# Four known experts in one job, and fewer rounded slots for the last main tiles, in a two-block transformer kernel with a mixture of experts

## The chip, the cores and the metric

One core of one Trainium2 chip runs the whole program. The metric is device time in microseconds (us) of one execution. TensorE (PE) multiplies, VectorE (DVE), ScalarE (ACT) and GpSimd (POOL) do the rest, and the queue of SyncE (SP) issues nearly all loads.

## The reference

Two blocks work on 256 tokens of width 1024. The first has two layers with feed-forward networks, a convolution mixer, an mLSTM mixer and cross attention. The second has a mixer with three branches, an output product, a layer norm, and then the part that matters here: a router, 16 experts of which each token takes two, and an embedding term gated by a product with `ple_gate`.

```
h = layer_norm_2(DEEPNORM_ALPHA_2 * h + y, ln1_g, ln1_b)        # y = merged @ w_out
e = (p @ ple_proj) * sigmoid(h @ ple_gate)
aff = sigmoid(h @ w_router)                                     # 16 columns
# the best of 4 groups of 4 experts, then the best 2 experts in it; weights from aff, normed
m = sum over the 2 experts of w * (silu(h @ gate_e) * (h @ up_e)) @ down_e
out = layer_norm_2(DEEPNORM_ALPHA_2 * h + m + e, ln2_g, ln2_b)
```

An expert has 1024 x 1024 floats of `gate` and `up` and 512 x 1024 of `down`. All is float32.

## The kernel before

**Main tiles.** All weights ahead of the experts come as a fixed list of tiles (`weight_tiles`), most of them 128 x 2048 floats, 1 MiB. SP loads tile `i` into one of four `raw` buffers (`load`). ScalarE rounds it into `whi` (`round_tile`) and VectorE makes the rest, `raw - whi`, in `wlo` (`rest_tile`), each in two halves; TensorE multiplies with both. There are four rounded slots, tile `i` in slot `i % 4`, and both engines wait before they write it until TensorE is through with tile `i - 4`. Rounding is called from a `Stream` that stands in each engine's own order of work and runs two or three tiles ahead.

The last main tiles are, in order: two of `mla_proj_2`, two of `conv_proj_2` (the second is `out2_0 - 1`), four of `w_out_2` (`out2_0` to `out2_0 + 3`) and `ple_proj_2`. The output product takes tile `out2_0`, then `+1`, each for both blocks of 128 tokens. Then it takes `+2` and `+3` together (`tail=True`): both for the first token block, then both for the second. For tile `out2_0 + j` it waits for `merged j`. VectorE makes these in pairs: in its order stand the rounding of tiles `out2_0 + 1` and `+2`, then the sums of columns 2 and 3, then `merged` 2 and 3, then the rounding of `+3` and of the `ple` tile.

**After the output product.** A layer norm in two token blocks gives `x`. TensorE turns block 0 (`turned(7, 0)`), multiplies the embedding (`embedded(t, n)`), and for the router turns block 1 and takes 16 columns (`affinities(t)`). VectorE's `route` picks experts, and `placing` finds each token's slot in its expert.

**Experts.** Four experts are known in advance (`FIXED`, columns 0 to 3, experts 12 to 15); the other twelve are ranked by their number of tokens at run time (columns 4 to 15). Each column has room for a fixed number of tokens (`ROOM`). If a column has more, a flag starts further passes over everything (`PASSES`); with these inputs the known ones have 22, 16, 23 and 27 tokens, the ranked ones 66, 51, 51, 45, 40, 36, 30, 27, 27, 26, 16 and 9. A job fills the 128 partitions with the slots of two or four experts (`PIECES`). For each job: `gather` brings its tokens' columns (for two jobs at a time), four `up` steps make gate and up products, then ScalarE's silu, VectorE's product (`gated`), a transpose (`turn_h`), a selection (`columns`), two `down` steps and two `scatter` steps back to the tokens. Between them stand four products `gate(c)` for the embedding. Products with experts of one job go to different columns of TensorE (64 or 32 each) and run side by side.

**Expert tiles.** Each expert has six tiles of 1 MiB (four for `up`, two for `down`), and there are four gate tiles. `expert_tiles` gives the order. They go round 15 slots (`wslots`), and four more slots are used once (`ONCE`). A slot's first load waits for what lay there (`wslot_after`), a later one for the step that used it (`used`). SP issues them in the order of its list and waits for each in turn; four go out in the middle of the last main tiles, the others after `merged 3`, behind the router's weights `wr`. The last norm's row `gbv` is the last load.

Of the kernel before, what the change touches and what calls it, by code (L numbers as in the profile page):

```python
# [10 lines left out]
D = 1024  # L11
T = 256
FF = 2816
NEXP = 16
# [6 lines left out]
TILE = 2048  # L21
# [102 lines left out]
NR, NS, LOOK, OPEN = 4, 4, 2, 0  # L124
# [4 lines left out]
RANKED = NEXP - FIXED  # L129
HALVES = [[(0, 64, q), (64, 128, q + 1)] for q in (0, 2, 5, 7, 9)]  # L130
PIECES = HALVES + [[(32 * i, 32 * i + 32, 4) for i in range(3)] + [(96, 128, 11)], [(32 * i, 32 * i + 32, 12 + i) for i in range(4)]]
ROOM = 4 * [64] + [96] + 6 * [64] + 5 * [32]
JOBS, PASSES = len(PIECES), 4
WSLOTS = 15
LATE = (2 * 512, 3 * 512, 4 * 512)
ONCE = (0, 8, 12, 17)
EROWS = 768
# [10 lines left out]
def group_jobs(G):  # L148
    return range(2 * G - 1, 2 * G + 1) if G else range(1)

# [168 lines left out]
def program(nc, A, out):  # L319
# [5 lines left out]
    with ctx:  # L325
# [80 lines left out]
        prior = [i - NR if i >= NR else None for i in range(main_tiles)]  # L406
        out2_0 = next(i for i, t in enumerate(tiles) if t[0] == "w_out_2")
        etiles = [expert_tiles(v == 0) for v in range(PASSES)]
        enumber = [{t: i for i, t in enumerate(tiles_)} for tiles_ in etiles]
# [106 lines left out]
        pTr = kT[:, 0, :, :]  # L516
        pp = blocks(ar[:, 0:2 * D], D)

        def held(i):
            return [hold[h * NS + i % NS][:, :] for h in range(2)]  # L520

        m4 = main_tiles - 4
        wslots = [ar[:, 2 * D + TILE * i:2 * D + TILE * (i + 1)] for i in range(3)]
        wslots += [raw[(m4 + i) % NR][:, :] for i in range(2)] + held(m4) + [raw[(m4 + 2 + i) % NR][:, :] for i in range(2)]
        wslots += held(m4 + 1) + held(m4 + 2) + held(m4 + 3)
        wslot_after = [None] * 3 + [("raw", m4), ("raw", m4 + 1)] + [("tile", m4)] * 2 + [("raw", m4 + 2), ("raw", m4 + 3)]
        wslot_after += [("tile", m4 + 1 + i) for i in range(3) for h in range(2)]
        assert len(wslots) == len(wslot_after) == WSLOTS
        wslots += [xe[:, 0, :, :].rearrange("p b n -> p (b n)"), r[:, :, :].rearrange("p t d -> p (t d)"), hs[:, :], gbv]

        arena = Arena(ar, 2 * D + 3 * TILE)
        sel16 = vm[:, :, :, :].rearrange("p a b n -> p (a b n)")[0:16].rearrange("p (q n) -> p q n", n=64)
# [41 lines left out]
        def tile_views(i):  # L574
            t = tiles[i]
            w, n = tile_width(t), t[5] - t[4]
            return blocks(whi[i % NS][:, 0:w], n), blocks(wlo[i % NS][:, 0:w], n)

# [17 lines left out]
        def tensor(e):  # L596
# [563 lines left out]
            embedded(0, 0)  # L1160
            embedded(0, 1)
            affinities(0)
            turned(7, 1)
            embedded(1, 0)
            affinities(1)
# [182 lines left out]
        def scalar(e):  # L1348
# [8 lines left out]
            def round_tile(i):  # L1357
                t = tiles[i]
                made = whi_made
                if i >= NS:  # L1360
                    need.wait_ge(*pe.at("tile", i - NS))
                for n in range(len(part_cuts(t)) - 1):
                    c0, c1 = part_cols(i, n)
                    if i == 0:
                        need.wait_ge(*xT_in[n].at("xT"))
                        copy(xhi[:, 2 * n:2 * n + 2, :], xTr[:, 2 * n:2 * n + 2, :]).then_inc(*act.up(("xhi", 0, n)))
                    need.wait_ge(*(piece_in[i][n] if i < 2 else raw_in[slot[i]]).at("raw", i))
                    copy(whi[i % NS][:, c0:c1], raw_t[slot[i]][:, c0:c1]).then_inc(*made.up((i, n)))

            w = Stream(round_tile, main_tiles)  # L1370

# [446 lines left out]
            tokens(0)  # L1818
            embedded(0, 1)
            turned(7, 1)  # L1820
            embedded(1, 0)
            tokens(1)
            need.wait_ge(*pe.at("bank", ("router",)))
            e.activation(aff, blocks(place["router",][:, 0:32], 16), ACT.Sigmoid).then_inc(*act.up(("aff",), took(("router",))))
            embedded(1, 1)
            normed(7)
            gate_part(0)

            def experts(v, s):
# [22 lines left out]
                def take(n, i):  # L1852
                    need.wait_ge(*s.pe.at("bank", ("ey", v, n, i)))
                    if n:
                        need.wait_ge(*s.pe.at("back", v, n - 1, i, 1))
                    if (v, n, i) == (0, 0, 0):
                        need.wait_ge(*pe.at("used", 0, 0, 5))
                    copy(y_hi[:, 512 * i:512 * i + 512], place["ey", v, n, i][:, :]).then_inc(*s.act.up(("yhi", v, n, i)))
# [53 lines left out]
        def vector(e):  # L1912
# [5 lines left out]
            def rest_tile(i):  # L1918
                hi_made, made = whi_made, wlo_made
                if i >= NS:  # L1920
                    need.wait_ge(*pe.at("tile", i - NS))
                for n in range(len(part_cuts(tiles[i])) - 1):
                    c0, c1 = part_cols(i, n)
                    if i == 0:
                        rest(xlo[:, 2 * n:2 * n + 2, :], xTr[:, 2 * n:2 * n + 2, :], xhi[:, 2 * n:2 * n + 2, :],
                             ("xhi", 0, n)).then_inc(*dve.up(("xT", 0, n)))
                    need.wait_ge(*hi_made.at(i, n))
                    e.tensor_tensor(wlo[i % NS][:, c0:c1], raw_t[slot[i]][:, c0:c1], whi[i % NS][:, c0:c1].bitcast(f32),  # L1928
                                    ALU.subtract).then_inc(*made.up((i, n)))

            w = Stream(rest_tile, main_tiles)

# [604 lines left out]
            def experts(v, s, part=range(JOBS + 1), amid=None):  # L2537
# [32 lines left out]
                def columns(n):  # L2570
                    need.wait_ge(*s.pe.at("bank", ("pbc", v, n)))
                    if n > 1:
                        need.wait_ge(*s.pe.at("back", v, n - 2, 1, 1))
                    i = 0 if n < len(HALVES) else n - len(HALVES) + 1
                    col = slot_col[:, i:i + 1]
                    e.tensor_scalar(tsel[:, n % 2, :], place["pbc", v, n][:, 0:256], col, None,
                                    ALU.is_equal).then_inc(*s.dve.up(("T", v, n), took(("pbc", v, n))))
# [160 lines left out]
        def gpsimd(e):  # L2738
# [92 lines left out]
            then(e.memset(roomT, 64.0))  # L2831
            for q in (4, *range(11, 16)):
                then(e.memset(room[:, q:q + 1], float(ROOM[q])))
# [3 lines left out]
            then(e.affine_select(out=roomT, in_=roomT, compare_op=ALU.is_ge, fill=32.0, base=10, pattern=[[0, 1]],  # L2837
                                 channel_multiplier=-1))
            pool.mark("roomT")
            then(e.memset(sel16, 0.0))  # L2840
# [14 lines left out]
        def sync(e):  # L2855
# [12 lines left out]
            def load_expert(v, i, late=None):  # L2868
# [7 lines left out]
                if g == ONCE[0]:  # L2876
                    need.wait_ge(*pe.at("bank", ("rstd",)))
                elif g == ONCE[1]:
                    need.wait_ge(*dve.at("centred", 7, 1))
                    need.wait_ge(*act.at("sq", 7, 1))  # L2880
                elif g == ONCE[2]:
                    need.wait_ge(*pe.at("tile", main_tiles - 1))
                elif g == ONCE[3]:
                    for t in range(2):
                        need.wait_ge(*dve.at("x", 7, t, 1))
                elif turn_of[g] >= WSLOTS:
                    v_, i_ = esequence[ring[turn_of[g] - WSLOTS]]
                    need.wait_ge(*(over if v_ else main).pe.at("used", v_, *[etiles[v_][i_][m] for m in (0, 2)]))
                elif wslot_after[turn_of[g]] is None:
                    need.wait_ge(*pe.at("bank", ("rstd",)))  # L2890
                elif wslot_after[turn_of[g]][0] == "raw":
                    i_ = wslot_after[turn_of[g]][1]
                    need.wait_ge(*wlo_made.at(i_, len(part_cuts(tiles[i_])) - 2))
                else:
                    need.wait_ge(*pe.at(*wslot_after[turn_of[g]]))
# [24 lines left out]
            for i in range(NR, main_tiles):  # L2920
# [15 lines left out]
                if i == out2_0:  # L2936
                    for n in range(4):
                        load_expert(0, n)
            need.wait_ge(*dve.at("merged", 3))
            e.dma_start(wr, blocks(A["wr"][:, :], NEXP)).then_inc(*router_in.up(("router",)))  # L2940
            for i in (*range(4, 8), 9, 10, 11, 13, 14, 8, 15, 17, 16, 18, 12, *range(19, len(etiles[0]))):
                load_expert(0, i)
            for late in range(2):
                for i in range(len(etiles[0]) - len(job_columns(JOBS - 1)), len(etiles[0])):
                    load_expert(0, i, late)
            n, _, j = etiles[0][ONCE[3]]
            need.wait_ge(*pe.at("used", 0, n, j))
# [141 lines left out]
```

## Time and profile before

| | us |
|---|---|
| median of 3 runs | 1460.66 (1460.21 to 1463.91) |
| profiled execution, its own time | 1460.58 |
| its span | 1458.8 |
| PE busy | 1426.8 (98%) |
| PE weight load busy | 1160.8 (80%) |
| DVE busy | 915.1 (63%) |
| ACT busy | 710.1 (49%) |
| POOL busy | 50.1 (3%) |

The span is from the first to the last instruction of one profiled execution; its own time is 1.8 us more. Busy times of engines overlap. In the chain that ended last, PE has 91% of the span and DVE 5%. The engines are told apart by stage below: an average over the span says little, since the transfers run at 229 GB/s in the mean and above 400 GB/s in the expert stage.

### The profile page before, as it was taken

To read this page: it belongs to the slowest core of one execution; us is meant where nothing else is said; L and a number is where in the kernel's file an instruction comes from. 1 tells how busy PE (TensorE), PEld (TensorE's weight loads), DVE (VectorE), ACT (ScalarE), POOL (GpSimd) and SP (SyncE) were. 2 spreads that over 40 slices of the span, in tenths; PEclk is the share of its full clock that TensorE was granted. 3 is DMA by queue.
4 is the path that set the end of the run, shared out by engine and by line. 5 is a ranking of instruction groups with operands and counts; after the bars stand their busy time and mean duration, and the time that the engine had idled before them with its cause. 6 is when DMAs were issued, how large, how long until landed. Compare 5 with 4: busy or idle time off the path is not lost.

```text
span 1458.8 us, 20739 instructions
## 1 busy us (share of the span) xinstructions
PE 1426.8 (98%) x8376; PEld 1160.8 (80%) x8376; DVE 915.1 (63%) x1510; ACT 710.1 (49%) x1185; POOL 50.1 (3%) x116
## 2 busy tenths in 40 slices
PE   8999999999999999999999999998999999999995
PEld 7888888888888988889888888888899997445441
DVE  7666678766666765566677656667989686121123
ACT  7445456455564554455754554545557663112111
POOL 0000000000000000000022000001000012000000
PEclk9999999999999999999999999999999999999998
DMA  9754554564545555545336645553563479999997
GB/s 345 279 202 173 190 205 154 202 231 174 195 180 188 210 183 207 194 148 180 135 116 245 251 176 182 193 175 133 177 202 117 144 303 409 388 412 421 417 421 296
DMA packets 50198, 333.78 MB, mean 229 GB/s; under 512 B 5808, under 2 KB 6064, under 8 KB 12208
## 3 DMA queue, kind: packets, MB, share of 16 engines
q1 hardware_dynamic: 48512, 322.55, 59.3%
q10 hardware_dynamic: 1584, 9.83, 1.8%
q8 instruction: 68, 1.11, 0.3%
q14 instruction: 34, 0.28, 0.1%
HBM read 331.31 MB, written 1.05 MB: 228 GB/s over the span
## 4 chain that ended last, share of the span: by engine, by line
PE 91%; DVE 5%; ACT 1%; DMA 1%; SPq 1%; POOL 1%; issue 0%; DVEq 0%; ACTq 0%
PE psw L602 56%; PE psy L602 33%; PE psw L605 2%; DVE wlo L1928 1%; SPq L2873 1%; DMA hold<-in_we 1%; POOL r L2790 0%; DVE x L2020 0%; DVE kT L2319 0%; DVE xs L1937 0%; ACT whi L1355 0%; ACT gb L1477 0%; DMA ar<-in_xT 0%; DVE r L2002 0%; DVE x L2033 0%
## 5 line engine op out<-in xcount | busy, mean ns | idle before, releaser
L602 PE MATMUL psw<-xs,whi 128*128 128x512 f32 (+2 forms) x2160 | 650.5, 366 | 6.5 <-DVE wlo L1928 6.4
L1928 DVE TENSOR_TENSOR wlo<-raw,whi 128x1024 fp32r<-128x1024 f32 (+4 forms) x415 | 476.8, 1192 | 77.6 <-ACT whi L1355 72.5
L602 PE MATMUL psw<-xs,wlo 128*128 128x256 f32 x1848 | 484.4, 280 | 0.0
L602 PEld LDWEIGHTS psw<-xs,whi 128*128 128x128 f32 (+1 forms) x2160 | 375.9, 189 | 61.8 <-DVE wlo L1928 6.4
L1355 ACT ACTIVATE whi<-raw 128x1024 fp32r<-128x1024 f32 (+4 forms) x415 | 402.3, 1024 | 7.7 <-PE psy L602 5.2
L602 PEld LDWEIGHTS psw<-xs,wlo 128*128 128x128 f32 x1848 | 350.3, 190 | 17.2
L1355 ACT ACTIVATE hf<-psw 128x256 f32<-128x256 f32 x90 | 34.1, 385 | 211.8 <-PE psw L602 211.7
L1973 DVE TENSOR_TENSOR hf<-hf,psw 128x256 f32<-128x256 f32 x82 | 34.0, 420 | 146.9 <-ACT hf L1355 146.9
L1355 ACT ACTIVATE ar<-psw 128x256 f32<-128x256 f32 (+2 forms) x141 | 60.0, 430 | 126.3 <-PE psw L602 124.3
L602 PE MATMUL psy<-whi,hhi 128*128 128x512 f32 x352 | 111.1, 390 | 0.0
L602 PE MATMUL psy<-wlo,hhi 128*128 128x512 f32 x352 | 111.0, 389 | 0.0
L602 PE MATMUL psy<-whi,hlo 128*128 128x512 f32 x352 | 111.0, 389 | 0.0
L602 PEld LDWEIGHTS psy<-wlo,hhi 128*128 128x128 f32 x352 | 66.1, 188 | 13.8
L602 PEld LDWEIGHTS psy<-whi,hlo 128*128 128x128 f32 x352 | 66.1, 188 | 13.8
L602 PEld LDWEIGHTS psy<-whi,hhi 128*128 128x128 f32 x352 | 66.1, 188 | 12.8 <-issue 0.2
L1980 DVE TENSOR_TENSOR ar<-ar,psw 128x256 f32<-128x256 f32 x82 | 34.2, 417 | 52.4 <-ACT ar L1355 52.4
L602 PE MATMUL psy<-hold,r 128*32 128x512 f32 (+1 forms) x272 | 52.1, 621 | 2.2 <-DMA hold<-in_we 2.2
L2748 POOL TENSOR_TENSOR rstd<-ve,mhalf 128x1 f32<-128x1 f32 x18 | 11.9, 662 | 1111.6 <-DVE ve L2026 1111.6
L2319 DVE SCALAR_TENSOR_TENSOR kT<-ar,par,kT 128x256 f32<-128x256 f32 x120 | 49.7, 477 | 0.0
L602 PE MATMUL psw<-whi,xs 128*128 128x256 f32 (+1 forms) x224 | 47.7, 302 | 0.6 <-DVE xs L1937 0.6
L602 PE MATMUL psy<-whi,xs 128*128 128x384 f32 (+1 forms) x192 | 45.1, 340 | 0.8 <-DVE xs L1937 0.8
L1355 ACT ACTIVATE hhi<-psw 128x512 fp32r<-128x512 f32 x17 | 10.0, 597 | 70.3 <-PE psw L602 64.8
(347 smaller groups left out, 1786.5 us busy)
## 6 DMA issues: line engine op xcount, KB each, us to landing
raw<-in_ws SPq DMA_DIRECT2D x189, 1024.0 KB, 4.8
hold<-in_we SPq DMA_DIRECT2D x47, 1024.0 KB, 10.9
raw<-in_we SPq DMA_DIRECT2D x22, 1024.0 KB, 9.5
ar<-in_we SPq DMA_DIRECT2D x20, 1024.0 KB, 10.9
gb<-in_ln ACTq DMA_DIRECT2D x7, 1024.0 KB, 5.0
raw<-in_ws SPq DMA_DIRECT2D x9, 768.0 KB, 4.3
raw<-in_ws SPq DMA_DIRECT2D x4, 672.0 KB, 4.0
raw<-in_ws SPq DMA_DIRECT2D x8, 256.0 KB, 7.0
```

The source lines that it names most:

```text
L602: return e.matmul(o, l, rr, start=start, stop=stop)
L605: return e.transpose(o, i, ident[0:n, 0:n])
L1355: return e.activation(o, i, ACT.Copy, **k)
L1928: e.tensor_tensor(wlo[i % NS][:, c0:c1], raw_t[slot[i]][:, c0:c1], whi[i % NS][:, c0:c1].bitcast(f32), ALU.subtract).then_inc(*made.up((i, ...
L1973: e.tensor_tensor(hf[:, s, j, :], hf[:, s, j, :], place["fgate", f, c, j][:, 0:256], ALU.add).then_inc(*dve.up(("fgate", f, c, j), took((" ...
L1980: then(e.tensor_tensor(corr[j], corr[j], place["up", f, c, j][:, 0:256], ALU.add), took(("up", f, c, j)))
L2319: ins = e.scalar_tensor_tensor(out=ca[:, b, :], in0=zc[:, b, tap:tap + 256], scalar=dwt[:, b, tap:tap + 1], in1=ca[:, b, :], op0=ALU.mult, ...
L2748: e.tensor_tensor(rstd[:, t:t + 1], ve[:, t:t + 1], mhalf[:, 0:1], ALU.pow).then_inc(*pool.up(("rstd", n, t)))
L2873: e.dma_start(wslots[at][:, c0:c1], A["we"][bass.ds(rows_of[q] + 128 * j, 128), c0:c1] if q in rows_of else A["we"][0:128, c0:c1]).then_in ...
```

## The change

The first job takes all four known experts, 32 slots each, in place of two jobs of two with 64 slots each. There are six jobs instead of seven, and their room shrinks with them. `PASSES` goes from 4 to 8. The rounded slots of the last main tiles are laid out by hand: `out2_0 + 2` takes the slot of `out2_0`, `+3` that of `+1`, the `ple` tile that of `out2_0 - 2`; the `ple` tile is rounded before `+3`. The slot of `out2_0 - 1` is then free for two expert tiles, and the embedding's product `pp` moves from `ar` into a used slot, so that `ar` holds four expert tiles instead of three. Five expert tiles are loaded early, four more follow before the wait for `merged 3`. The router's two products stand one behind the other.

```diff
+PIECES = [quarters(0), halves_of(5), halves_of(7), halves_of(9), [(32 * i, 32 * i + 32, 4) for i in range(3)] + [(96, 128, 11)], quarters(12)]
+KIND = (2, 0, 0, 0, 1, 2)
+ROOM = 4 * [32] + [96] + 6 * [64] + 5 * [32]
+JOBS, PASSES = len(PIECES), 8
...
-ONCE = (0, 8, 12, 17)
+ONCE = (0, 14, 15, 16)
+EARLY_SLOTS = 5
...
+        m_ple = out2_0 + 4
+        hslot, hprior = [i % NS for i in range(main_tiles)], [i - NS if i >= NS else None for i in range(main_tiles)]
+        spare = hslot[out2_0 + 3]
+        for i, taken in ((out2_0 + 2, out2_0), (out2_0 + 3, out2_0 + 1), (m_ple, out2_0 - 2)):
+            hslot[i], hprior[i] = hslot[taken], taken
+        making = list(range(main_tiles))
+        making[out2_0 + 3], making[m_ple] = m_ple, out2_0 + 3
...
+        pp = blocks(held(hslot[out2_0 + 2])[0], D)
+        wslots = [ar[:, TILE * i:TILE * (i + 1)] for i in range(4)] + held(spare)
+        wslots += [raw[slot[i]][:, :] for i in (out2_0 + 1, out2_0 + 2, m_ple, out2_0 + 3)]
+        wslots += [held(hslot[out2_0 + 2])[1], *held(hslot[out2_0 + 3]), *held(hslot[m_ple])]
+        wslot_after = [None] * 4 + [("tile", out2_0 - 1)] * 2 + [("raw", i) for i in (out2_0 + 1, out2_0 + 2, m_ple, out2_0 + 3)]
+        wslot_after += [("tile", out2_0 + 2), ("tile", out2_0 + 3), ("tile", out2_0 + 3), ("tile", m_ple), ("tile", m_ple)]
...
+            embedded(1, 0)
+            turned(7, 1)
             affinities(0)
-            turned(7, 1)
-            embedded(1, 0)
             affinities(1)
             embedded(1, 1)
...
                 if i >= NS:
-                    need.wait_ge(*pe.at("tile", i - NS))
+                    need.wait_ge(*pe.at("tile", hprior[i]))
...
-                    copy(whi[i % NS][:, c0:c1], raw_t[slot[i]][:, c0:c1]).then_inc(*made.up((i, n)))
+                    copy(whi[hslot[i]][:, c0:c1], raw_t[slot[i]][:, c0:c1]).then_inc(*made.up((i, n)))
...
-            w = Stream(round_tile, main_tiles)
+            w = Stream(lambda i: round_tile(making[i]), main_tiles)
...
             embedded(1, 1)
+            tokens(1)
...
-            for q in (4, *range(11, 16)):
+            for q in (*range(5), *range(11, 16)):
                 then(e.memset(room[:, q:q + 1], float(ROOM[q])))
...
+            then(e.affine_select(out=roomT, in_=roomT, compare_op=ALU.is_ge, fill=32.0, base=-4, pattern=[[0, 1]],
+                                 channel_multiplier=1))
...
                 if i == out2_0:
-                    for n in range(4):
+                    for n in range(EARLY_SLOTS):
                         load_expert(0, n)
-            need.wait_ge(*dve.at("merged", 3))
-            e.dma_start(wr, blocks(A["wr"][:, :], NEXP)).then_inc(*router_in.up(("router",)))
-            for i in (*range(4, 8), 9, 10, 11, 13, 14, 8, 15, 17, 16, 18, 12, *range(19, len(etiles[0]))):
+            for i in range(EARLY_SLOTS, len(etiles[0])):
+                if i == EARLY_SLOTS + 4:
+                    need.wait_ge(*dve.at("merged", 3))
+                    e.dma_start(wr, blocks(A["wr"][:, :], NEXP)).then_inc(*router_in.up(("router",)))
                 load_expert(0, i)
```

VectorE's `rest_tile` changes as ScalarE's `round_tile` does. The new helpers `quarters(q)` and `halves_of(q)` give the pieces of a job of four and of two experts.

## Rows read from the trace of the kernel before

**Rows 1.** Windows: stretch, length, each engine's busy time, clock, DMA share, GB/s.
```profile
1234.60:1280.00 45.40, 45.40 (x248) 19.00 (x246) 8.94 (x28) 5.76 (x10) 0.00 (x0) 1.00 0.96 378
1280.00:1420.00 140.00, 140.00 (x864) 63.52 (x860) 28.64 (x54) 25.02 (x35) 0.00 (x0) 1.00 1.01 420
1420.00:1446.00 26.00, 18.64 (x122) 6.34 (x120) 5.71 (x11) 1.79 (x3) 0.00 (x0) 0.87 1.01 406
```

**Rows 2.** Chain of waits, expert stage: start, duration, what.
```profile
1297.14 2.06 PE psw L602 x8
1299.20 7.02 PE psy L602 x32
1306.22 0.59 PE psw L605 x4
1306.81 3.58 PE psy L602 x16
1310.39 7.59 PE psw L602 x36
...
1434.98 10.65 DMA hold<-in_we
```

**Rows 3.** Timeline of the SP queue: start, duration of the group, issues.
```profile
1163.02 0.33 SPq L2911 DMA_DIRECT2D xe<-in_wg  x1
1163.39 1.71 SPq L2911 DMA_DIRECT2D ar<-in_we  x3
1165.14 17.52 SPq L2864 DMA_DIRECT2D raw<-in_ws  x4
1195.30 0.33 SPq L2940 DMA_DIRECT2D ar<-in_wr  x1
...
1220.43 0.43 SPq L2911 DMA_DIRECT2D hs<-in_we  x1
1234.60 4.74 SPq L2911 DMA_DIRECT2D ar<-in_we  x3
```

**Rows 4.** Timeline of TensorE, one `up` step of four experts (two records each).
```profile
1370.15 3.64 PE L602 MATMUL psy<-hold,r 128*32 128x512 f32 x32
```

**Rows 5.** Windows, columns as in rows 1: transfers starting from an empty queue.
```profile
1163.00:1165.50 2.50, 2.50 (x23) 2.50 (x23) 1.22 (x1) 2.47 (x5) 0.00 (x0) 1.00 0.57 134
```

**Rows 6.** Timeline of ScalarE: rounding of `+1` and `+2`; copies of block 1's transpose.
```profile
1185.53 3.89 ACT L1355 ACTIVATE whi<-raw 128x1024 fp32r<-128x1024 f32 x4
...
1213.65 1.09 ACT L1355 ACTIVATE xe<-psw 128x512 f32<-128x512 f32 x2 [1.09 <-PE psw L605]
```

**Rows 7.** Timeline of TensorE: start of tile `+2`, and the first transpose after the product.
```profile
1196.76 0.62 PE L602 MATMUL psy<-whi,mhi 128*128 128x512 f32 x2
...
1207.65 1.03 PE L605 MATMUL psw<-par,x 128*128 128x128 f32 x8
```

**Rows 8.** Timeline of VectorE: roundings, `merged` 2 and 3, and `pick(0)`.
```profile
1186.61 4.63 DVE L1928 TENSOR_TENSOR wlo<-raw,whi 128x1024 fp32r<-128x1024 f32 x4 [0.26 <-ACT whi L1355]
...
1193.80 1.47 DVE L1937 TENSOR_TENSOR mlo<-ar,mhi 128x512 fp32r<-128x512 f32 x2
...
1196.06 4.63 DVE L1928 TENSOR_TENSOR wlo<-raw,whi 128x1024 fp32r<-128x1024 f32 x4 [0.18 <-ACT whi L1355]
...
1225.54 0.74 DVE L2551 TENSOR_SCALAR gsel<-ar 128x64 fp32r<-128x64 f32 x4
```

**Rows 9.** Timeline of TensorE: 8 router products as 16 records, and the first gather.
```profile
1211.28 1.85 PE L602 MATMUL psy<-ar,xe 128*128 128x16 f32 x16
...
1227.10 0.52 PE L602 MATMUL psw<-gsel,mhi 128*128 128x128 f32 x2
```

**Rows 10.** Last job: two of TensorE's waits (in brackets), and the clock after the first.
```profile
1424.74 5.29 PE L602 MATMUL psy<-hold,r 128*32 128x512 f32 x32 [2.24 <-DMA hold<-in_we]
1431.63 0.63 PE L605 MATMUL psw<-par,hf 128*128 128x128 f32 x4 [1.59 <-DVE hf L2567]
...
1424.70:1428.10 3.40, 3.36 (x16) 0.90 (x20) 0.00 (x0) 0.00 (x0) 0.00 (x0) 0.50 1.01 419
```

More of the change, by code:

```diff
@@ L129, with quarters, halves_of @@
 RANKED = NEXP - FIXED
[L130 to L133, printed above, removed]
+def quarters(q):
+    return [(32 * i, 32 * i + 32, q + i) for i in range(4)]
+def halves_of(q):
+    return [(0, 64, q), (64, 128, q + 1)]
+PIECES = [quarters(0), halves_of(5), halves_of(7), halves_of(9), [(32 * i, 32 * i + 32, 4) for i in range(3)] + [(96, 128, 11)], quarters(12)]
+KIND = (2, 0, 0, 0, 1, 2)
+ROOM = 4 * [32] + [96] + 6 * [64] + 5 * [32]
+JOBS, PASSES = len(PIECES), 8
 WSLOTS = 15
 LATE = (2 * 512, 3 * 512, 4 * 512)
-ONCE = (0, 8, 12, 17)
+ONCE = (0, 14, 15, 16)
+EARLY_SLOTS = 5
 EROWS = 768
@@ L148, in group_jobs @@
 def group_jobs(G):
-    return range(2 * G - 1, 2 * G + 1) if G else range(1)
+    return range(2 * G - 1, min(2 * G + 1, JOBS)) if G else range(1)
 def group_of(n):
@@ L516, in program, with held @@
         pTr = kT[:, 0, :, :]
[L517 to L527, printed above, removed]
+        def held(k):
+            return [hold[h * NS + k][:, :] for h in range(2)]
+        pp = blocks(held(hslot[out2_0 + 2])[0], D)
[4 more added lines that the diff above has]
+        wslot_after += [("tile", out2_0 + 2), ("tile", out2_0 + 3), ("tile", out2_0 + 3), ("tile", m_ple), ("tile", m_ple)]
         assert len(wslots) == len(wslot_after) == WSLOTS
-        wslots += [xe[:, 0, :, :].rearrange("p b n -> p (b n)"), r[:, :, :].rearrange("p t d -> p (t d)"), hs[:, :], gbv]
-        arena = Arena(ar, 2 * D + 3 * TILE)
+        wslots += [xe[:, 0, :, :].rearrange("p b n -> p (b n)"), r[:, :, :].rearrange("p t d -> p (t d)"), gbv, hs[:, :]]
+        arena = Arena(ar, 4 * TILE)
         sel16 = vm[:, :, :, :].rearrange("p a b n -> p (a b n)")[0:16].rearrange("p (q n) -> p q n", n=64)
@@ L576, in tile_views @@
             w, n = tile_width(t), t[5] - t[4]
-            return blocks(whi[i % NS][:, 0:w], n), blocks(wlo[i % NS][:, 0:w], n)
+            return blocks(whi[hslot[i]][:, 0:w], n), blocks(wlo[hslot[i]][:, 0:w], n)
         def part_cols(i, n):
@@ L1819, in scalar @@
             embedded(0, 1)
+            embedded(1, 0)
             turned(7, 1)
-            embedded(1, 0)
-            tokens(1)
             need.wait_ge(*pe.at("bank", ("router",)))
@@ L1855, in take @@
                         need.wait_ge(*s.pe.at("back", v, n - 1, i, 1))
-                    if (v, n, i) == (0, 0, 0):
-                        need.wait_ge(*pe.at("used", 0, 0, 5))
                     copy(y_hi[:, 512 * i:512 * i + 512], place["ey", v, n, i][:, :]).then_inc(*s.act.up(("yhi", v, n, i)))
@@ L1920, in rest_tile @@
                 if i >= NS:
-                    need.wait_ge(*pe.at("tile", i - NS))
+                    need.wait_ge(*pe.at("tile", hprior[i]))
                 for n in range(len(part_cuts(tiles[i])) - 1):
@@ L1927, in rest_tile @@
                     need.wait_ge(*hi_made.at(i, n))
-                    e.tensor_tensor(wlo[i % NS][:, c0:c1], raw_t[slot[i]][:, c0:c1], whi[i % NS][:, c0:c1].bitcast(f32),
+                    e.tensor_tensor(wlo[hslot[i]][:, c0:c1], raw_t[slot[i]][:, c0:c1], whi[hslot[i]][:, c0:c1].bitcast(f32),
                                     ALU.subtract).then_inc(*made.up((i, n)))
-            w = Stream(rest_tile, main_tiles)
+            w = Stream(lambda i: rest_tile(making[i]), main_tiles)
             def rest(lo, src, hi, event, scale=None):
@@ L2573, in columns @@
                         need.wait_ge(*s.pe.at("back", v, n - 2, 1, 1))
-                    i = 0 if n < len(HALVES) else n - len(HALVES) + 1
-                    col = slot_col[:, i:i + 1]
+                    col = slot_col[:, KIND[n]:KIND[n] + 1]
                     e.tensor_scalar(tsel[:, n % 2, :], place["pbc", v, n][:, 0:256], col, None,
@@ L2881, in load_expert @@
                 elif g == ONCE[2]:
-                    need.wait_ge(*pe.at("tile", main_tiles - 1))
-                elif g == ONCE[3]:
                     for t in range(2):
                         need.wait_ge(*dve.at("x", 7, t, 1))
+                elif g == ONCE[3]:
+                    need.wait_ge(*pe.at("tile", m_ple))
                 elif turn_of[g] >= WSLOTS:
@@ L2945, in sync @@
                     load_expert(0, i, late)
-            n, _, j = etiles[0][ONCE[3]]
+            n, _, j = etiles[0][ONCE[2]]
             need.wait_ge(*pe.at("used", 0, n, j))
```

## The prediction

> **What bounds the kernel now.** I read the profile from its end backwards. The windows come first [rows 1]: from 1280 us to 1420 us TensorE is busy throughout and the DMA engines are full as well, at 420 GB/s; after 1420 us TensorE is busy 18.64 us of 26 us while the DMA engines stay full to 1446 us. Two resources run side by side, and the reader should see which of them ends last. The chain of waits says it [rows 2]: the last long piece before the final norm is the landing of a `hold` slot, 1434.98 us plus 10.65 us. So the end is set by the transfers: the last expert tile lands near 1445.6 us, and some 13 us of products, norm and store follow.
>
> When can that last tile land? The expert stage loads 16 x 6 expert tiles and 4 gate tiles of 1 MiB (1.049 MB) and the last norm's row, and they go through 15 + 4 slots. The queue's own issues [rows 3] show three epochs: four tiles at 1163 us, nothing between 1182 us and 1195 us, then fifteen tiles to 1220.43 us, which fill every slot, and no issue until 1234.60 us. At that time TensorE has ended its first `up` step (`used 0, 0, 0`) and gives its slots back. I call this time F: 19 tiles are in, 81 and the norm's row are to come. From F the transfers need 82 x 1.049 = 86.0 MB at 420 GB/s, 204.7 us, and yet they end 211.4 us after F. The windows give the rest [rows 1]: 378 GB/s instead of 420 over 45.4 us is 4.5 us, 406 instead of 420 over the last 26 us is 0.9 us, and about 1.3 us are what was still in flight at F (378 x 45.4 + 420 x 140 + 406 x 26 us are 86.5 MB, 0.5 MB over the 86.0). The 4.5 us are slots given back two at a time, each `up` step of a two-expert job freeing two tiles in 3.5 us while the queue could load 1.4, and then none while TensorE gathers.
>
> **The change part by part.**
>
> *One job of four instead of two of two.* 32 columns of TensorE per expert in place of 64: four such products side by side take 3.64 us for an `up` step [rows 4], what two 64-column ones take (3.58 us, [rows 2]). So a whole job goes: four `up` steps, two `down`, a transpose, a selection and a scatter, 7.02 + 3.58 + 3.58 + 7.59 + 0.59 + 2.06 = 24.4 us of TensorE. Taken at face value it is the largest term. I cost it at nothing, since it lies under the transfers, whose bytes don't change: TensorE will wait for tiles some 24 us more. Its other effect counts. Each `up` step of the first job now frees four tiles, 10 us of loading, in 3.6 us. Following the queue from F: after 3 steps 12 slots are back, and the `gather` that follows finds 10 tiles to load. The 4.5 us of thin transfers go. The other end of this term: half stays, 2.2 us.
>
> *Five early tiles, and more behind them before `merged`.* Slots then fill with the tiles before it (`spare` from `out2_0 - 1`, ended near 1186 us), and the hole between 1182 us and 1195 us takes three or four tiles. Laid out by their events, 19 tiles are in by about 1232 us instead of 1234.6 us. But the slots number 19 as before, so the queue stops again until F. Worth nothing unless F is earlier, and it costs a fresh start: the queue is empty at F. A start from empty is seen at 1163 us [rows 5]: 134 GB/s over 2.5 us, a loss of 1.7 us. The Trainium skill, "DMA: Bandwidth & Descriptors", section on the anatomy of one DMA, has about 2.0 us fixed per transfer; by that the sum would be 0.3 us more, and the trace roughly agrees. The main loads behind the fifth early tile land 2.5 us later, near 1180 us; the first of them is rounded at 1185.53 us [rows 6], so that is covered. If the cover went, ScalarE's rounding would be late, then VectorE's.
>
> *Rounded slots shared.* This adds a wait. Tile `out2_0 + 2` is now rounded into the slot of `out2_0`, and ScalarE must wait until TensorE is through with that tile: tile `+1`'s 24 products, 0.227 us each, are over when `+2` begins at 1196.76 us, so they begin at 1191.3 us and the last of `out2_0` ends near 1191.5 us [rows 7]. Before, its copies were part of four in 3.89 us from 1185.53 us, done by 1189.4 us [rows 6]. Now: start 1191.6 us, halves done at 1192.6 and 1193.6 us, VectorE's halves (4.63 us for four, 1.16 each, [rows 8]) done at 1195.05 us instead of 1191.24 us, 3.8 us late. Behind it on VectorE's queue stand the merges of columns 2 and 3, and TensorE waits for these: `merged 2` came at 1194.54 us (first half of the pair at 1193.80 us, [rows 8]), now at 1198.35 us; TensorE comes for it at 1196.76 us [rows 7]. Stall one, 1.6 us. Then 12 products (48 stand between 1196.76 and 1207.65 us, [rows 7]), to 1201.1 us. Tile `+3` now stands behind the `ple` tile in the order of rounding. VectorE began the four halves at 1196.06 us, now at 1199.86 us, and `+3` has the third and fourth: 1203.4 and 1204.5 us. Stall two, 2.3 us, and 0.4 us more before the second half. The first token block ends at 1206.6 us instead of 1202.2 us. The norm, the router and the first gather follow without slack on TensorE, so F moves by 4.4 us, to 1238.9 us. Bounds: 1.6 us if the second stall is hidden, 6.1 us if the clock falls (below).
>
> *Router's products in one go.* The same products in another order. Before, an `embedded` product covers ScalarE's copy of the second block's transpose; afterwards the first 8 products of the router do (1.85 us, [rows 9]), longer than the two copies together (1.09 us, [rows 6]). Nothing, with 0.2 us either way. `tokens(1)` moves behind ScalarE's sigmoid; VectorE wants it only after routing. Four more `gsel` pieces in `pick(0)` are 0.74 us on VectorE (four took 0.74 us from 1225.54 us, [rows 8]), ready at about 1227.05 us, while TensorE comes for them at 1227.10 us [rows 9]: nothing, at most 0.1 us. GpSimd's four extra memsets and one select end long before their readers. In the last job `enriched` now lies between `gated` and the last selection on VectorE, two adds as wide as a rounding half, 1.2 us each; the selection is wanted only after the last `down` product, which waits for its tile. Eight passes in place of four lengthen only code that isn't entered.
>
> **The sum.** F goes from 1234.5 to 1238.9 us. From there: start from empty 1.7, 204.7 for 86.0 MB, 0.9 for the ragged last 26 us; the transfers end at 1446.2 us, against 1446.0 us. What follows is the same. So the profiled execution's own time of 1460.58 us, 14.6 us after the transfers' end, gives 1460.8 us; the median of the runs shown, 1460.66 us, is 0.1 us above it and changes nothing.
>
> **The rivals.**
>
> *TensorE was the bound* (chance 0.04). For it: busy without a gap to 1420 us [rows 1]. Then 24.4 us go: 1436 us. Against it: the bytes. The transfers can't end before 1234.5 + 204.7 us less the 1.3 us in flight, 1437.9 us, so even with F unmoved and nothing lost the time is 14.6 us later, 1452.5 us.
>
> *The rounding wait is hidden, wholly or half* (0.14). If `merged 2` and tile `+3` come in time, F stays at 1234.5 us and the recovered 4.5 us count alone: 1456.4 us; with the first stall only, 1458.0 us. The order of VectorE's queue speaks against it.
>
> *One fall of the clock* (0.16). TensorE's granted clock is 1.00 here (2.4 GHz), but it fell to 0.50 (1.2 GHz) from 1424.7 us to 1428.1 us after an idle time of 2.24 us, and did not at once after one of 1.59 us [rows 10]; 32 products then took 5.29 us instead of 3.64 us, 1.7 us more. The two new stalls are 1.6 and 2.3 us. One such fall gives 1462.5 us.
>
> *The slower one: the clock stays low through the output product and the router* (0.12). TensorE has 11 us of products left at 1196.76 us and 19 us more to the first gather's start, all on the path to F. Each microsecond at half clock costs half a microsecond. It decides from 8.5 us of low clock on (4.2 us, 1465 us); low until 1215 us would give 1469 us. For it: three stalls close together. Against it: the fall in [rows 10] lasted 3.4 us and ended as soon as TensorE was busy.
>
> *The early slots do what they are for and F doesn't matter*: that is, TensorE had been waiting for tiles at 1231 us. The rows show no gap there [rows 9], so it has no chance of its own.
>
> **How the numbers follow.** The forecast has 0.54 (1458.5 to 1463 us by its bounds: half of the thin transfers staying gives 1463.0 us, a shorter second stall 1458.5 us). A change within 0.3%, some 4.4 us, can't be told from none. Faster: TensorE the bound, a third of the hidden-wait case, and 0.04 of my own errors in F, 0.13. Slower: the low clock, 0.12, and 0.03 for a fall together with the thin transfers, 0.15. The range from 1456.2 to 1465.0 us leaves out those two groups, in part.
>
> **What would show it.** Right: TensorE stalls near 1196.8 and 1201 us; the first `up` step ends near 1239 us; no issues between about 1223 and 1239 us; then 420 GB/s without a dip to the end; TensorE's busy time 24 us less and as much more waiting for `raw`, `hold` and `ar` landings. Wrong: no stall in the output product, a first `up` ending near 1234.5 us, a clock below 1.00 before 1239 us, or transfers that thin out again after it.

## The result, and the profile after

The changed kernel takes 1464.7 us (median of 6 runs, 1463.06 to 1467.48) against 1460.62 us, a ratio of 1.0030 with a 95% interval of 1.0019 to 1.0041. It is slower by 4.1 us, inside the range but not in the forecast case. The profiled execution took 1466.34 us; the median lies 1.6 us below it.

The queue's issues in the changed kernel (timeline of SP, columns as in [rows 3]):

```profile
1164.61 0.33 SPq L2925 DMA_DIRECT2D xe<-in_wg  x1
1164.98 2.22 SPq L2925 DMA_DIRECT2D ar<-in_we  x4
1167.24 17.02 SPq L2878 DMA_DIRECT2D raw<-in_ws  x4
1187.64 0.80 SPq L2925 DMA_DIRECT2D hold<-in_we  x2
1190.59 6.40 SPq L2925 DMA_DIRECT2D raw<-in_we  x2
1200.70 0.33 SPq L2956 DMA_DIRECT2D ar<-in_wr  x1
...
1226.46 0.91 SPq L2925 DMA_DIRECT2D hold<-in_we  x2
1244.46 2.07 SPq L2925 DMA_DIRECT2D ar<-in_we  x4
```

Four tiles go out before `merged 3` that did not before, the slots are full from 1227 us on, and then nothing goes out until the first `up` step ends: F is 1244.46 us, where [rows 3] have 1234.60 us. I call X the issue of the first early load; it waits for the same product in every kernel here, so F - X tells the path from there to F without what happened before it. It was 1234.60 - 1163.02 = 71.58 us and is 79.85 us, 8.3 us more; the other 1.6 us of F came before X.

TensorE in that stretch (timeline; the wait ahead of a line in brackets), answering to [rows 7, 9]:

```profile
1200.03 0.70 PE L617 MATMUL psy<-whi,mhi 128*128 128x512 f32 x2 [1.52 <-DVE mlo L1950]
...
1205.01 0.62 PE L617 MATMUL psy<-whi,mhi 128*128 128x512 f32 x1 [1.97 <-DVE wlo L1941]
...
1220.93 3.64 PE L617 MATMUL psy<-ar,xe 128*128 128x16 f32 x32
...
1231.65 1.54 PE L617 MATMUL psw<-ar 128*128 128x16 f32 x10 [1.28 <-DVE ar L2503]
...
1236.95 0.52 PE L617 MATMUL psw<-gsel,mhi 128*128 128x128 f32 x2
...
1240.76 3.64 PE L617 MATMUL psy<-ar,xe 128*32 128x512 f32 x32
```

Both forecast stalls are there, for `merged 2` and for the rounding of tile `+3`, of 1.52 and 1.97 us (1.6 and 2.3 were forecast). ScalarE and VectorE show where they come from (timelines of both, to be read beside [rows 6, 8]):

```profile
1193.11 2.01 ACT L1370 ACTIVATE whi<-raw 128x1024 fp32r<-128x1024 f32 x2 [4.00 <-PE psy L617]
...
1194.27 2.36 DVE L1941 TENSOR_TENSOR wlo<-raw,whi 128x1024 fp32r<-128x1024 f32 x2 [3.71 <-ACT whi L1370]
...
1199.20 1.47 DVE L1950 TENSOR_TENSOR mlo<-ar,mhi 128x512 fp32r<-128x512 f32 x2
...
1201.45 4.63 DVE L1941 TENSOR_TENSOR wlo<-raw,whi 128x1024 fp32r<-128x1024 f32 x4 [0.18 <-ACT whi L1370]
```

ScalarE stands 4.00 us waiting for TensorE to be through with `out2_0`, and everything behind it on VectorE is late by 3.8 us (the two merges start 34.59 us after X, before 30.78 us). What was not in the forecast case are the lines of the clock (windows, columns as in rows 1, the last but two is the granted clock):

```profile
1205.20:1208.60 3.40, 3.40 (x9) 2.43 (x9) 1.58 (x3) 0.00 (x0) 0.00 (x0) 0.50 0.90 316
1219.00:1225.00 6.00, 6.00 (x48) 5.53 (x47) 2.61 (x4) 2.66 (x6) 4.83 (x21) 1.00 1.01 423
...
1232.50:1236.00 3.50, 3.50 (x11) 2.96 (x12) 2.90 (x17) 0.00 (x0) 0.00 (x0) 0.51 0.77 325
```

It fell twice to 1.2 GHz, each time for 3.4 us. The first fall began at 1205.2 us, right behind the second stall. The second began at 1232.5 us. The router's products had ended 8.0 us earlier, with the clock still at 1.00; in between TensorE had waited 1.28 us for VectorE's routing and had begun ten small products. The sum, from the table of stages below: 4.6 us of stalls and late rounding, 1.1 us for the first fall, 0.9 us more from the first transpose to the routing's product (0.7 us of it waiting, 1.28 us for 0.56 us), 1.7 us for the second fall. That is the 8.3 us.

From F on the forecast nearly holds. Windows of the expert stage, beside [rows 1], and the end of the chain of waits, beside [rows 2]:

```profile
1244.40:1280.00 35.60, 34.02 (x284) 14.85 (x278) 8.23 (x27) 4.67 (x8) 0.00 (x0) 1.00 0.98 403
1280.00:1420.00 140.00, 128.27 (x772) 59.75 (x772) 21.40 (x42) 22.42 (x33) 0.00 (x0) 0.98 1.01 421
```

```profile
1440.50 10.80 DMA hold<-in_we
1451.31 0.14 issue
1451.44 1.10 PE psw L617 x8
```

The transfers now run at 403 GB/s in the first 35.6 us (421 would have saved 1.5 us, the start from an empty queue; 1.7 was forecast) where 378 stood. The last tile lands at 1451.3 us, 206.8 us after F (207.3 forecast). The execution ends 221.9 us after F, against 226.0 us before. So in this profile the job of four gave back 4.1 us, and the path to F took 8.3 us. TensorE's waits confirm who paces whom (waits of TensorE after 1244 us: total, times, longest; first the kernel before, then the changed one):

```profile
PE psy L602 <- DMA hold<-in_we: 2.2, 1, 2.2
PE psw L602 <- DMA ar<-in_we: 1.9, 1, 1.9
```

```profile
PE psy L617 <- DMA hold<-in_we: 10.6, 4, 5.0
PE psw L617 <- DMA ar<-in_we: 3.9, 3, 1.8
PE psy L617 <- DMA raw<-in_we: 2.8, 3, 1.3
PE psy L617 <- DMA ar<-in_we: 2.1, 2, 1.3
```

TensorE is busy 20.1 us less from F on (186.3 us for 206.3 us), where 24 us were forecast. A fall of the clock of 6.8 us at 1396.4 us, which the kernel before doesn't have, makes up to 3.4 us of the difference.

### The profile page after: what moved, and what is told of

It is laid out like the page before. It is cut to its first block, busy times and chain, and to the rows that moved or that the text cites. A ratio compares the mean times of both kernels' runs of the same rounds, so it can differ in the third digit from the quotient of the medians.

```text
span 1464.5 us, 20705 instructions
## 1 busy us (share of the span) xinstructions
PE 1412.2 (96%) x8364; PEld 1156.9 (79%) x8364; DVE 911.2 (62%) x1502; ACT 706.9 (48%) x1181; POOL 50.5 (3%) x121
## 3 DMA queue, kind: packets, MB, share of 16 engines
HBM read 331.31 MB, written 1.05 MB: 227 GB/s over the span
## 4 chain that ended last, share of the span: by engine, by line
PE 84%; DMA 6%; DVE 5%; SPq 2%; ACT 2%; POOL 1%; issue 1%; DVEq 0%; ACTq 0%
PE psw L617 53%; PE psy L617 29%; DMA ar<-in_we 3%; DMA raw<-in_we 2%; DVE wlo L1941 2%; PE psw L620 1%; SPq L2887 1%; DMA hold<-in_we 1%; SPq L2925 1%; ACT whi L1370 0%; POOL r L2802 0%; DVE x L2033 0%; DVE kT L2332 0%; DMA raw<-in_ws 0%; DVE xs L1950 0%
## 5 line engine op out<-in xcount | busy, mean ns | idle before, releaser
L1370 ACT ACTIVATE whi<-raw 128x1024 fp32r<-128x1024 f32 (+4 forms) x415 | 402.4, 1024 | 13.4 <-PE psy L617 9.2
L617 PE MATMUL psy<-hold,xe 128*32 128x512 f32 (+2 forms) x216 | 50.4, 532 | 0.7 <-DMA hold<-in_we 0.7
```

Of the source, the lines that this page charges most:

```text
L617: return e.matmul(o, l, rr, start=start, stop=stop)
L1370: return e.activation(o, i, ACT.Copy, **k)
```

## The experiments

All profiles, in one table. Times in us; "low" is how long TensorE's granted clock was 0.50 between X and F, in falls. In the expectations theory A is my account at that point, and the other letters are rivals.

| kernel | median | ratio, 95% | X | F | F - X | low | own time - F |
|---|---|---|---|---|---|---|---|
| before | 1460.6 | 1 | 1163.02 | 1234.60 | 71.58 | none | 226.0 |
| changed | 1464.7 | 1.0030, 1.0019 to 1.0041 | 1164.61 | 1244.46 | 79.85 | 3.4 + 3.4 | 221.9 |
| e10, changed again | one run, 1463.73 | | 1161.68 | 1240.41 | 78.73 | 3.4 | 223.3 |
| e1 jobs only | 1457.39 | 0.9981, 0.9971 to 0.9992 | 1163.89 | 1235.28 | 71.39 | none | 222.1 |
| e2 slots and router only | 1465.79 | 1.0048, 1.0034 to 1.0062 | 1160.98 | 1237.29 | 76.31 | none | 227.1 |
| e11, e2 again | one run, 1465.11 | | 1161.70 | 1238.84 | 77.14 | 3.4 | 226.3 |
| e3 natural order | 1461.97 | 1.0012, 1.0003 to 1.0021 | 1163.46 | 1238.33 | 74.87 | 3.4 | 223.2 |
| e4 other slots | 1459.66 | 0.9995, 0.9986 to 1.0004 | 1164.90 | 1237.44 | 72.54 | 3.4 | 223.2 |
| e5 other slots, old router | 1458.87 | 0.9988, 0.9979 to 0.9997 | 1162.18 | 1233.57 | 71.39 | none | 223.4 |
| e6 changed, old router | 1460.86 | 1.0006, 0.9995 to 1.0016 | 1161.57 | 1237.53 | 75.96 | none | 221.9 |
| e7 router only | 1463.66 | 1.0020, 1.0010 to 1.0029 | 1163.17 | 1237.35 | 74.18 | 6.8 | 225.9 |
| e8 as e5, four early tiles fewer | 1456.55 | 0.9975, 0.9966 to 0.9983 | 1161.54 | 1232.93 | 71.39 | none | 223.1 |
| e9 router split | 1461.68 | 1.0012, 1.0003 to 1.0021 | 1162.38 | 1235.17 | 72.79 | none | 226.3 |

Ratios are to runs of the kernel before on the same chip. X differs by up to 3.9 us from profile to profile, for nothing that these kernels change. It goes with how long the clock is low near 714 us: not at all in six profiles (X from 1160.98 to 1162.18), 3.4 us in five (1162.38 to 1163.89), 6.8 us in two (1164.61 and 1164.90).

The last column splits at the landing of the last tile. That comes 206.8 to 207.3 us after F in all eight profiles with the job of four, 211.0 us in the kernel before. What follows takes 15.0 us in three of the eight (changed, e1, e6) and 16.1 to 16.3 us in the other five, whose clock is 0.50 to 0.53 over the 12 us behind the landing, where the three have 0.77 to 0.78. So the job's gain up to the landing is the steady part, 3.7 to 4.2 us.

The stages of the path, in us after X (TensorE's timelines): the start of tile `+2`, the first transpose behind the output product, the routing's ten products, the first gather, and F.

| kernel | `+2` | transpose | routing's products | gather | F |
|---|---|---|---|---|---|
| before | 33.74 | 44.63 | 60.45 | 64.08 | 71.58 |
| e5 | 33.75 | 44.63 | 60.27 | 63.89 | 71.39 |
| e4 | 33.75 | 44.64 | 61.52 | 65.03 | 72.54 |
| e6 | 35.43 | 49.20 | 64.84 | 68.46 | 75.96 |
| e10 | 35.43 | 49.20 | 65.92 | 71.22 | 78.73 |
| changed | 35.42 | 50.33 | 67.04 | 72.34 | 79.85 |

**e1, the jobs alone.** The kernel before with the new `PIECES`, `KIND`, `ROOM`, `JOBS` and `PASSES`, and what hangs on them (GpSimd's memsets, the choice of the job's kind, one wait of ScalarE less):

```diff
-HALVES = [[(0, 64, q), (64, 128, q + 1)] for q in (0, 2, 5, 7, 9)]
...
+PIECES = [quarters(0), halves_of(5), halves_of(7), halves_of(9), [(32 * i, 32 * i + 32, 4) for i in range(3)] + [(96, 128, 11)], quarters(12)]
+ROOM = 4 * [32] + [96] + 6 * [64] + 5 * [32]
```

> The job of four known experts and the smaller room alone; rounded slots, early loads and the router's order stay as in the kernel before. Theory A (the job gives back the 4.5 us of thin transfers, the rounding wait and the clock take more than that): no stall in the output product, first up step over at 1234.5 us, transfers at 420 GB/s from there to the end, 1456 us (4.5 us faster than before). Rival B (TensorE, now waiting for tiles all along, loses to the clock or to late tiles in the expert stage, and that is the loss): 1461 us or more, with the last tile no earlier than 1446 us.

Measured: 0.9981, 2.8 us faster in the ratio, F - X unchanged, 222.1 us after F instead of 226.0 us. Windows of e1 from F:

```profile
1235.20:1280.00 44.80, 40.94 (x317) 17.08 (x308) 8.99 (x28) 5.27 (x9) 0.00 (x0) 1.00 1.01 413
```

413 GB/s stand where [rows 1] have 378. Theory A holds, though the gain is 1.7 us less than expected in the ratio and 0.6 us less in the profile. Rival B is out as the cause of the loss: TensorE waits for tiles all along here, and the kernel is faster. Waiting isn't always free, though: see the 1.2 us at the end in five of the eight profiles above.

**e2, the slots and the router without the jobs.** `PIECES`, `ROOM` and `PASSES` of the kernel before in the changed kernel; the four once-used slots go to the tiles that allow it with these jobs, and the order of the loads follows.

```diff
-ONCE = (0, 14, 15, 16)
+ONCE = (0, 8, 17, 12)
```

> The shared rounded slots, the five early tiles and the router's order, with the jobs of the kernel before. Theory A: the two stalls (1.5 and 2.0 us seen in the changed kernel) and two falls of the clock in front of the first up step, and the thin transfers of two-expert jobs stay: 1466 to 1469 us. Rival B (the expert stage is at fault): near 1461 us.

Measured: 1465.79 us, just under the range expected, and 7 us slower in the ratio; F - X is 4.7 us up and 227.1 us follow. But the profile shows no fall of the clock, only the two stalls (1.5 and 2.0 us), which left open how the falls come about. A second profile was taken later (e11).

**e3, tile `+3` rounded ahead of the `ple` tile again.**

```diff
-        making[out2_0 + 3], making[m_ple] = m_ple, out2_0 + 3
```

> The changed kernel with the output product's fourth tile rounded before the ple tile again. Theory A: the stall before the second tile pair's product stays (1.5 us), the other (2.0 us and a bit) goes, 2.4 us off the path, and 0 to 3.4 us more if a fall of the clock goes with it: 1459 to 1462.3 us. Rival B: no difference to the changed kernel, 1464.7 us.

Measured: 1461.97 us. The stall for `merged 2` stays (1.5 us), that for tile `+3` shrinks to 0.2 us, and one fall of 3.4 us is left. F - X is 5.0 us below the first profile of the changed kernel and 3.9 us below the second (e10). Theory A.

**e4, other slots.** Tile `+2` keeps the slot of `out2_0 - 2`, `+3` takes that of `out2_0`, `ple` that of `+1`; the spared slot is the same.

```diff
-        for i, taken in ((out2_0 + 2, out2_0), (out2_0 + 3, out2_0 + 1), (m_ple, out2_0 - 2)):
+        for i, taken in ((out2_0 + 2, out2_0 - 2), (out2_0 + 3, out2_0), (m_ple, out2_0 + 1)):
```

> The changed kernel with other rounded slots for the last tiles: the third output tile keeps the slot of the tile two before the first, the fourth takes that of the first, the ple tile that of the second; the same slot is spared for two early expert tiles, and the order of rounding is the natural one. Theory A: no stall in the output product, no fall of the clock there, first up step over at 1234.5 to 1235 us, 1456 to 1457 us. Rival B: stalls go but the time stays at 1464 us, or falls by the 4 us of the stalls alone, 1460.5 us.

Measured: 1459.66 us, 3 us above what theory A gave. The stalls are gone, as the theory has it, but a fall is there without them, behind the router's products, which here end at 1219.2 us. Windows of e4:

```profile
1213.00:1219.20 6.20, 6.20 (x49) 5.73 (x48) 2.58 (x3) 3.06 (x6) 5.09 (x21) 1.00 1.00 416
1219.20:1222.60 3.40, 3.40 (x9) 2.62 (x9) 2.81 (x13) 0.99 (x3) 2.41 (x12) 0.50 0.72 296
```

TensorE was busy 6.20 us of the 6.20 us ahead of the fall. This is where my theory fell short: the clock falls here without any idle time, and the one edit left between the stalls and F was the router's order. It had been priced at nothing. The fall itself costs next to nothing here, though. From the first transpose to the routing's products e4 takes 16.88 us and e10, whose clock is full in that part, takes 16.72 us; e5, with the old order, takes 15.64 us. In e10 TensorE ends that part with a wait of 1.28 us, in e4 the slower clock fills it. So of the 1.15 us that separate e4's F - X from e5's, 1.1 us are a longer way to the routing's result and not the clock.

**e5, e6 and e7, the router's order.** The old order put into e4 (e5) and into the changed kernel (e6), and the new order put into the kernel before (e7). The edit of e5 and e6 (ScalarE's order of `tokens(1)` and the copies goes back with it, and moves with it in e7):

```diff
-            embedded(1, 0)
-            turned(7, 1)
             affinities(0)
+            turned(7, 1)
+            embedded(1, 0)
             affinities(1)
             embedded(1, 1)
```

> The kernel with the other rounded slots (no stall in the output product), and the router's products and ScalarE's order there as in the kernel before. Theory A (two blocks of thin router products in one go let TensorE's clock fall, 1.7 us): no fall between 1163 us and the first up step, that step over 71.5 us after the first early load as in the kernel before (72.5 us with the products in one go), 1457.5 us. Rival C (the fall there came by chance, or from something else in the new order of slots): a fall near 1220 us all the same, 1459.7 us.

> The changed kernel with the router's products as in the kernel before. Theory A: the stalls of 1.5 and 2.0 us and the fall behind them stay, the fall at 1232 us goes: 1463 us, 1.7 us below the changed kernel; first up step over 78 us after the first early load (79.9 us in the changed kernel). Rival C: 1464.7 us.

> The kernel before with nothing changed but the order of the router's products and of ScalarE's work there. Theory A: TensorE's queue of work is as long as before, but the clock falls once behind the products: 1462.3 us, first up step over 73.3 us after the first early load (71.6 us in the kernel before). Rival C (order costs nothing): 1460.7 us and no fall.

Measured: none of the two with the old order has a fall between X and F; F - X is 71.39 us in e5, and 75.96 us in e6, where the stalls are left. e6 is at 1460.86 us, 3.8 us below the changed kernel, more than the 1.7 us expected: both falls and most of the wait for the router went (1.28 us to 0.38 us). The first of the two falls lies ahead of the router, and e10 doesn't have it either, so the order can't be credited with that one. (One of e6's 12 runs took 6735.67 us, which nothing here explains. The median counts it, the ratio doesn't; the other 11 have a median of 1460.30 us.) The intervals of e6 and the changed kernel don't overlap, those of e4 and e5 do. e7 adds 2.6 us to F - X and is slower by 0.20%. Windows of e7:

```profile
1210.00:1216.70 6.70, 6.70 (x48) 5.98 (x47) 3.00 (x5) 4.32 (x8) 4.81 (x16) 1.00 1.03 429
1216.70:1223.50 6.80, 6.80 (x20) 5.63 (x20) 4.57 (x22) 1.74 (x3) 3.19 (x12) 0.50 1.01 417
1223.50:1230.00 6.50, 6.50 (x37) 5.85 (x35) 4.01 (x19) 0.00 (x0) 0.00 (x0) 1.00 1.01 421
```

The fall begins while the products run (they start at 1213.80 us) and lasts 6.8 us, twice what was expected.

**e9, the transposes moved, the products apart.** The kernel before with the order `turned(7, 1)`, `affinities(0)`, `embedded(1, 0)`, `affinities(1)`.

```diff
-            affinities(0)
             turned(7, 1)
+            affinities(0)
             embedded(1, 0)
             affinities(1)
```

> The kernel before with the second block's transpose ahead of both router products and one embedding product between the two; ScalarE's order as in the changed kernel. Theory A (it is the unbroken stretch of thin products that lets the clock fall): no fall between 1163 us and the first up step, which is over 71.6 us after the first early load, 1461 us. Rival E (the moved transpose or ScalarE's new order is at fault, not the stretch): a fall near 1217 us or a later end without one, 74 us, 1463 us.

Measured: no fall. It is 0.12% slower all the same, for another reason, which its timeline of TensorE shows:

```profile
1211.84 1.32 PE L605 MATMUL psw<-par,x 128*128 128x128 f32 x8 [1.05 <-DVE x L2033]
1213.00 1.86 PE L602 MATMUL psy<-ar,xe 128*128 128x16 f32 x16
```

TensorE waits 1.05 us for the norm's `x`, and F - X is 1.2 us up. So neither pure theory: the fall goes with the unbroken stretch, but the transposes' place has a price of its own, which the changed kernel avoids by moving `embedded(1, 0)` ahead of them.

**e10 and e11, second profiles** of the changed kernel and of e2.

> The changed kernel as it is, for a second profile. Theory A: two stalls of 1.5 and 2.0 us in the output product, at least one fall of the clock between the stalls and the first up step, which is over 78 to 80 us after the first early load. Rival C (the falls of the first profile were chance): none, 76 us.

> The shared rounded slots with the old jobs, for a second profile, since the first showed the stalls but no fall. Theory A: the same stalls; a fall in this one is as likely as not, so 76.3 us or 78 us after the first early load. Rival C: 76.3 us again.

Measured: e10 has the same stalls, a wait of 1.28 us and one fall, from 1228.9 us; none behind the stalls. e11 has a fall from 1221.5 us, just behind the products, where e2 had none. So falls vary from execution to execution. Of seven profiles with the products in one go six have one or two between X and F; of six without, none, and one of those six (e6) has both stalls. Only the fall at 1205.2 us in the first profile of the changed kernel lies ahead of the products; five profiles have both stalls, and it is the only fall right behind them.

Six of seven overstates it, however. In four of the seven (e3, e4, e7, e11) the fall begins during the products or within 1.0 us of their end. In both profiles of the changed kernel it begins 8.0 and 8.4 us after their end, at the routing's products, behind the wait of 1.28 us (timeline of TensorE, e10):

```profile
1227.60 1.29 PE L617 MATMUL psw<-ar 128*128 128x16 f32 x10 [1.28 <-DVE ar L2503]
```

No run has that wait without the products in one go, so which of the two, or whether both, set off this fall stays open.

**e8, four early tiles fewer.** e5 with the wait for `merged 3` after five tiles instead of nine.

```diff
-                if i == EARLY_SLOTS + 4:
+                if i == EARLY_SLOTS:
```

> As the first kernel of this set (other rounded slots, router as before), but only five expert tiles go out ahead of the wait for merged 3 instead of nine. Theory A (slots, not their time, limit what lies in before the first up step ends): same time as that kernel within 0.7 us, rather below it since the queue is still full when the first slot comes back: 1457 us. Rival D (early tiles count by their bytes): four tiles of 2.5 us later, up to 10 us slower.

Measured: 1456.55 us, 0.25% faster than the kernel before and the fastest of all. F - X is 71.39 us as in e5, and the issues show the same stop before F (timeline of SP, e8):

```profile
1193.88 0.33 SPq L2955 DMA_DIRECT2D ar<-in_wr  x1
...
1217.52 1.60 SPq L2924 DMA_DIRECT2D hold<-in_we  x2
1232.93 2.08 SPq L2924 DMA_DIRECT2D ar<-in_we  x4
```

Rival D is out: tiles loaded earlier into the same number of slots bring nothing. The expectation was wrong in one point, the queue is as empty at F as in e5: 141 and 138 GB/s in the 2.5 us from F. Between e5 and e8 the profiles differ by 0.3 us after F, the medians by 2.3 us with intervals that overlap. e8's runs fall into two groups, six from 1454.88 to 1456.55 us and five from 1458.23 to 1459.31 us, and its median is the upper end of the first, so most of the 2.3 us need no cause; the rest is open.

## Why the prediction was wrong

*What bounds the kernel, and the job of four.* Right. The transfers pace the end; 24.4 us of TensorE's work bought nothing as such, and of the 4.5 us of thin transfers 3.7 to 4.2 us came back by the landing of the last tile, and 2.8 us (1.2 to 4.2) in the runs of e1.

*Early tiles worth nothing, start from empty 1.7 us.* Right: 1.5 us, and e5 against e8 for the early tiles (both start from empty).

*Rounded slots shared, 4.4 us.* Right in place, order and size: 1.52 and 1.97 us, and 4.6 us on F - X in e6 against e5 (75.96 and 71.39 us), where nothing else differs up to F but the slots and the order of rounding.

*Router's products in one go: "Nothing, with 0.2 us either way".* This is the step that failed. The sum counted what the products wait for and for how long they run, and both came out as forecast: 32 records in 3.64 us, twice 1.85 us less a little. But with the old order in its place the changed kernel takes 1460.86 us (e6), where 1460.8 us was forecast, and its F - X is 75.96 us, the 71.58 us of before and the 4.4 us forecast. The new order added 2.8 us to that in e10: 1.1 us because the routing's result comes later after the first transpose, and 1.7 us because the clock falls at the routing's products. In the first profile the fall behind the stalls, which is not the order's, comes on top with 1.1 us. Alone in the kernel before the new order costs 2.6 us on F - X and 0.20% in the runs (e7), there nearly all by a fall of 6.8 us: in e2, with the same order and no fall, the way from the first transpose to the routing's products is only 0.2 us longer than in the kernel before.

*One fall of the clock (0.16), and the slower rival (0.12).* The price of a fall, 1.7 us for 3.4 us, is right only where TensorE waits for nothing afterwards: the later fall of the changed kernel cost 1.7 us, its first 1.1 us, e11's 0.8 us (against e2), e4's 0.1 us. There the slower clock filled time in which TensorE would have waited. The cause of a fall was looked for in the new stalls alone, since the rows had falls after idle time. The argument that the fall in [rows 10] "ended as soon as TensorE was busy" misreads them: TensorE was busy 3.36 us of its 3.40 us. e6 and e4 part the two: stalls without the products in one go, no fall; the products without stalls, a fall. The forecast case, with no fall, should not have been the likeliest.

*The wait for the router* grew from 0.56 to 1.28 us in both profiles of the changed kernel; the prediction had it at nothing, and GpSimd's extra memsets and select too. Two of VectorE's small operations in the routing chain are stretched there, while GpSimd works on `vm`; in the kernel before it was one. GpSimd's and VectorE's timelines of the changed kernel:

```profile
1226.63 0.94 POOL L2854 MEMSET vm<- 16x1024 f32 x1
1227.71 1.14 POOL L2855 TENSOR_SCALAR_AFFINE_SELECT vm<-vm 16x1024 f32<-16x1024 f32 x1
...
1226.71 0.89 DVE L2494 TENSOR_SCALAR ar<-ar 128x8 f32<-128x8 f32 x1
...
1227.86 1.03 DVE L2499 TENSOR_TENSOR ar<-ar 128x32 f32<-128x32 f32 x1
```

Operations of those shapes take 0.17 and 0.19 us elsewhere in the same chain. In all 13 profiles one operation of the chain is stretched, to between 0.67 and 1.04 us, and it ends 0.02 to 0.05 us after GpSimd's select on `vm`. The second, the `TENSOR_SCALAR`, is stretched in the four profiles that have both the job of four and the new order (changed, e10, e3, e4), where it starts 0.08 or 0.09 us into GpSimd's memset of `vm` and ends 0.03 to 0.04 us after it. With the old order it begins ahead of the memset, or in its last 0.1 us; with the new order but without the extra memsets (e2, e11, e7) it begins after it. So it takes both parts of the change to get the 0.7 us. That the overlap is the cause is argued from the rows only; no run moved GpSimd's work by itself. `enriched` and the longer skipped code cost nothing, as forecast.

## What to carry to other kernels

When transfers pace a stage and its slots are full, look for what gives back the first slot: only that time counted here, not how early the slots were filled, and not TensorE's work behind it. A shared buffer is paid for by what stands behind the waiting engine in its order; giving the wait to the tile with the most slack (e4's slots) cost nothing for the same memory. And an order of work on one engine that looks free, since no product gets longer, still has to be priced: by when the others get their inputs, by what their operations then overlap, and by the clock. Here thin products (16 columns) in one unbroken stretch saved nothing and cost 2.6 to 2.8 us on the path in e7 and e10.

## What the runs showed of the hardware

TensorE's granted clock fell to 1.2 GHz without any idle time, behind 3.6 us of products with 16 columns (e4: 6.20 us busy of 6.20 us, then 0.50 for 3.4 us) or during them (e7: 0.50 for 6.8 us). It did so in four of seven profiles with such a stretch (e3, e4, e7, e11), and in none of six where two stretches of 1.85 us stood apart. The Trainium skill, "TensorE: Matmul & The Clock Gate", section on HAM oscillation, puts such falls down to idle gaps; these rows show one with none.

The same kernel shows a fall in one profile and not in the next: e11 has one behind the products and e2 none, and the clock is low near 714 us for 0, 3.4 or 6.8 us, with X at most 1162.18 us without it and at least 1164.61 us with 6.8 us of it. What a fall costs depends on the waits behind it: 1.7 us for 3.4 us of low clock where there is none, 0.1 us in e4, where a wait of 1.28 us takes it up.

A small VectorE operation of 0.17 to 0.20 us took 0.67 to 1.04 us when it lay beside GpSimd's select on 16 x 1024 floats, in every profile.
